# Cross attention's key products: five quarters moved from the span levels into the block attention

## The chip, the cores and the metric

One core of one Trainium2 chip runs the program. The metric is the device time of one execution in microseconds (us). Engines are named as in the profile: PE is TensorE's matmul side (PEld its weight loads), DVE is VectorE, ACT is ScalarE, POOL is GpSimd and SP is SyncE, which here issues the large weight transfers.

## What is computed

Two transformer blocks run one after the other over 256 tokens of width 1024. The first has a forgetting attention, an RWKV mixer and a mixture of 64 experts. The second has a token mixer of four groups (an mLSTM, a short convolution, a block attention called MoBA, and an HGRN2 recurrence), a cross attention over 256 memory tokens, and a gated feed-forward. The change lies in the second block. What matters of the reference:

```python
# token mixer of the second block: four independent groups of 256 columns
h_m = mlstm_chunkwise(...)                       # y_m
y_c = c_b * causal_dwconv(c_c * c_h, sconv_w)
y_a = moba_attention(a_q, a_k, a_v, rel_bias)    # 4 heads of 64, softmax over 256 keys
o_h = hgrn2_chunkwise(q_h, k_h, log_f, h_i)      # y_h
y   = concatenate([y_m, y_c, y_a, y_h]) @ w_out

# cross attention: k and v depend on the memory alone, not on x
q = xn @ wq
k = memn @ wk      # 256 x 512: the "key products"
v = memn @ wv      # 256 x 512
```

The keys `k` and values `v` of the cross attention need only the normalised memory and their weights. They can be computed at any time before the cross attention's scores, and the kernel uses them as work for PE while other groups wait for each other.

## The kernel before, in words

Every engine has one hand-written instruction stream, and semaphores order them. Nothing is reordered at run time: what stands first in an engine's stream holds up all that stands behind it. In the stretch of interest PE runs, in this order:

1. The mLSTM's heads (`weights`, `weighted`), then the transposes of the block attention's queries and keys.
2. **The block attention.** `moba_scores(h)` makes the scores of head h (two products with the head's keys, two that add the bias; 8 matmul records). `moba_attend(h)` issues five identity products (`keep_warm(5, 0)`, whose results nobody reads), waits for the exponentials of head h (`w_exp`, from ACT), transposes the three probability tiles, issues two more identity products, waits for DVE's copy of the transposes (`tp_evac`) and multiplies with the values. The scores of head h+1 are issued ahead of `moba_attend(h)`. On DVE, head h+1's scores are copied (L3254), two maxima are taken (L3256, L3257), and then the transposes of head h are copied (`moba_copy`, L3247). ACT takes the exponentials (L1178, L1180).
3. **The span levels** of HGRN2, eight of them (levels 0 to 7; `LEVELS` is 7). In each level PE issues `span_sums(level + 1)` (L2095), one quarter of the key or value products, the four transposes of the level's rows (L1361; they wait for DVE's `ft_src`), another quarter, and, once DVE has copied the transposes to `fT` (L3113), the level's products (L2120, L2122 in level 7). In each level DVE copies the transposes (L3113), makes the rows of the next level (`level_source`: L3279, L3284), does a piece of other work (`beside_level`: convolution taps, convolution sums, the mLSTM's norm and gate) and adds the masked products (L3308, L3310, twice each). ACT takes one exponential per level (`span_exp`, L1188).
4. The mixing products over `w_mix_out` (L1334), and later the cross attention.

`keys_values_part(n)` is one of sixteen quarters: n from 0 to 3 make the first half of the keys (`(J_CK, 0)`), 4 to 7 the second half, 8 to 11 and 12 to 15 the two tiles of the values (`J_CV`). A quarter is four matmuls over half of the depth, shown as 8 records of 256 columns (L1976, keys) or 4 of 512 (L1334, values). The first quarter of an output waits for its bank to be copied out (`lin_evac`) and, for keys and values each once, for their weights (`w_full`). ACT copies the finished outputs out of PSUM with `lin_copy_heads` (keys) and `lin_copy` (values). The ring of weights has two slots: SP loads `w_mix_out`'s first half into the slot of `w_ck` once the keys are done, and its second half into the slot of `w_cv` once the values are.

A score bank (`score_bank`, banks 6 and 7), a transpose bank (4 and 5) and the output banks 2 and 3 aren't touched by the quarters, which go to banks 0 and 1. The identity products go to bank 0.

Of the kernel before, what the change touches and what calls it, by code (L numbers as in the profile page):

```python
# [141 lines left out]
def build(nc, A, consts, out):  # L142
# [22 lines left out]
    with ctx:  # L165
# [222 lines left out]
        ckT = silu_c[:, :, :].rearrange("p (h b) c -> p h (b c)", h=CH)  # L388
# [221 lines left out]
        outputs = {}  # L610
# [20 lines left out]
        J_CK, J_CV, J_MIX = (J_OUT + 2 + i for i in range(3))  # L631
# [33 lines left out]
        def lin_bank(o):  # L665


            first = outputs[(J_OUT, 0)]
            if first <= o < first + 2 * T:
                return o - first  # L670
            return o % 2 + 6 * (o in [outputs[(("row", i), 0)] for i in range(N_ROWS)])

        def after(j, t=0):

            return outputs[(j, t)] + 1
# [155 lines left out]
        def _(act):  # L831
# [21 lines left out]
            def rstd(dst, src):  # L853

                rstd_n[0] += 1
                act.wait_ge(inv_var, rstd_n[0])
                act.activation(dst, src, ACT.Sqrt).then_inc(rstd_done, 1)

            def lin_copy(j, t, dst):
                act.wait_ge(lin_mm, after(j, t))  # L860
                act.activation(dst, bank[lin_bank(outputs[(j, t)])][:, 0:jobs[j][2]], ACT.Copy).then_inc(lin_evac, 1)

            def lin_copy_heads(j, i, dst):

                act.wait_ge(lin_mm, after(j, i))
                act.activation(dst[:, 2 * i:2 * i + 2, :],
                               bank[outputs[(j, i)] % 2][:, :].rearrange("p (h c) -> p h c", h=2), ACT.Copy)\
                    .then_inc(lin_evac, 1)
# [41 lines left out]
            for t in range(T):  # L910
                act.wait_ge(lin_mm, after(J_LORA, t))
                b = bank[lin_bank(outputs[(J_LORA, t)])]
                lo, n = IN_JOBS[J_LORA]
# [216 lines left out]
            for i in range(N_IN2):  # L1130
# [3 lines left out]
                for t in range(T):  # L1134
                    act.wait_ge(lin_mm, after(("in2", i), t))
                    n = in2_width(i)
# [46 lines left out]
            def span_exp(level):  # L1183

                act.wait_ge(decay_mm, GH + level + 1)
                if level >= 2:
                    act.wait_ge(ft_src, level - 1)
                act.activation(ex2[:, level % 2, :], bank[2 + level % 2][:, :], ACT.Exp).then_inc(hg_exp, 1)  # L1188

            span_exp(0)  # L1190
            for level in range(LEVELS + 1):
                if level < LEVELS:
                    span_exp(level + 1)
                if level in (1, 3):
                    lin_copy_heads(J_CK, level // 2, ckT)
                if level == 5:
                    rstd(ms[:, 12, :], ms[:, 11, :])
                if level in (5, 7):
                    lin_copy(J_CV, level // 2 - 2, cv[:, level // 2 - 2, :])
# [111 lines left out]
        def _(pe):  # L1311
# [5 lines left out]
            def keep_warm(n, b, lo=0, width=P):  # L1317

                for _ in range(n):
                    pe.matmul(bank[b][:, lo:lo + width], cst["ident"][:, :], cst["ident"][:, 0:width],  # L1320
                              start=True, stop=True, skip_group_check=True)

            def dense_tile(j, t, lhs, tiles=T, bias=False, part=(0, 1), bank_free=False):


                kind, lo, n, kt, parts, _ = jobs[j]
                if t == 0 and part[0] == 0:
                    full[j % RING] += 16 * len(parts)
                    pe.wait_ge(w_full[j % RING], full[j % RING])
                o = outputs[(j, t)]  # L1330
                if o >= 2 and part[0] == 0 and not bank_free:
                    pe.wait_ge(lin_evac, o - 1)
                for k in range(kt * part[0] // part[1], kt * (part[0] + 1) // part[1]):
                    mm = pe.matmul(bank[lin_bank(o)][:, 0:n], lhs(k, t), ring[:, j % RING, k * n:(k + 1) * n],  # L1334
                                   start=(k == 0), stop=(k == kt - 1 and not bias))
                if part[0] < part[1] - 1:
                    return
                if bias:
                    mm = pe.matmul(bank[lin_bank(o)][:, 0:n], ones[0:1, :],
                                   ring[0:1, j % RING, KT * BANK:KT * BANK + n], start=False, stop=True)  # L1340
                mm.then_inc(lin_mm, 1)
# [600 lines left out]
            for u in range(2, 2 * N_IN2):  # L1942
# [19 lines left out]
                if u % 2 == 0:  # L1962
                    mm.then_inc(in_done, 1)

            def dense_T_quarter(j, i, quarter):

                h, first = quarter // 2, quarter % 2 * KT // 2
                o = outputs[(j, i)]
                if quarter == 0:
                    if i == 0:  # L1970
                        full[j % RING] += 16 * len(jobs[j][4])
                        pe.wait_ge(w_full[j % RING], full[j % RING])
                    pe.wait_ge(lin_evac, o - 1)
                for k in range(first, first + KT // 2):
                    lo = k * CW + (2 * i + h) * CHD
                    mm = pe.matmul(bank[o % 2][:, h * 2 * P:(h + 1) * 2 * P], ring[:, j % RING, lo:lo + CHD],  # L1976
                                   xT[:, k, :], start=(k == 0), stop=(k == KT - 1))
                if quarter == 3:
                    mm.then_inc(lin_mm, 1)

            def keys_values_part(n):

                i, quarter = n // 4, n % 4
                if i < 2:
                    dense_T_quarter(J_CK, i, quarter)
                else:
                    dense_tile(J_CV, i - 2, xTk, part=(quarter, 4))
# [24 lines left out]
            n = tp_n[0]  # L2012
# [45 lines left out]
            def moba_scores(h):  # L2058
                b = score_bank()
                pe.matmul(b[:, 0:P], head_of(qT2, h, 0, P), head_of(kT2, h, 0, P), start=True, stop=False)  # L2060
                pe.matmul(b[:, 0:P], cst["anti"][:, :], hankel[:, h, P:2 * P], start=False, stop=True)
                pe.matmul(b[:, P:3 * P], head_of(qT2, h, P, 2 * P), head_of(kT2, h), start=True, stop=False)
                pe.matmul(b[:, P:3 * P], cst["anti"][:, :], hankel[:, h, :], start=False, stop=True).then_inc(sc_mm, 1)

            def moba_attend(h):
                keep_warm(5, 0)
                pe.wait_ge(w_exp, GH + h + 1)
                transposes([(i * P, (i + 1) * P, P, pr2[:, h % 2, i * P:(i + 1) * P]) for i in range(3)])
                keep_warm(2, 0)
                pe.wait_ge(tp_evac, TP_P2 + h + 1)  # L2070
                c = slice(h * HD, (h + 1) * HD)
                v = lambda t: z2[:, t, A_V + h * HD:A_V + (h + 1) * HD]
                w = lambda i: wT2[:, h % 2, i * P:(i + 1) * P]
                pe.matmul(bank[2][:, c], w(0), v(0), start=True, stop=True)
                pe.matmul(bank[3][:, c], w(1), v(0), start=True, stop=False)
                pe.matmul(bank[3][:, c], w(2), v(1), start=False, stop=True).then_inc(o_mm, 1)

            moba_scores(0)
            pe.wait_ge(o_used, 1)
            for h in range(GH):  # L2080
                if h + 1 < GH:
# [20 lines left out]
            for level in range(LEVELS + 1):  # L2102
                if level < LEVELS:
                    span_sums(level + 1)
                keys_values_part(2 * level)
                pe.wait_ge(ft_src, level + 1)
                transposes([((2 * pair + t) * P, (2 * pair + t + 1) * P, P,
                             level_rows[level % 2][:, t, pair * P:(pair + 1) * P])
                            for pair in range(2) for t in range(T)])
                keys_values_part(2 * level + 1)  # L2110
                pe.wait_ge(tp_evac, TP_HG + level + 1)
                for parity in range(2):
                    b = score_bank()
                    r = slice(HD * parity, HD * parity + HD)
                    for pair in range(2):
                        if level < LEVELS:
                            for t in range(T):
                                i = 2 * pair + t
                                f = fT[r, pair, t * P:(t + 1) * P]
                                mm = pe.matmul(b[:, i * P:(i + 1) * P], f, f, start=True, stop=True)  # L2120
                        else:
                            mm = pe.matmul(b[:, pair * P:(pair + 1) * P], fT[r, pair, 0:P], fT[r, pair, P:2 * P],  # L2122
                                           start=True, stop=True)
                    mm.then_inc(sc_mm, 1)
# [1372 lines left out]
```

## Time and profile before

| | us |
|---|---|
| Median of 3 runs | 1439.46 (1436.92 to 1439.6) |
| Profiled execution, its own time | 1441.09 |
| Its span in the trace | 1438.5 |
| PE busy in the span | 1352.1 (94%) |
| DVE busy | 640.7 (45%) |
| ACT busy | 364.2 (25%) |
| Chain that ended last, shares of the span | PE 82%, DVE 11%, DMA 3%, issue 2%, ACT 2% |

The span is what the trace covers; the profiled execution took 2.6 us more than its span. All start times below count from the span's start. The block attention lies at 1063 to 1084 us and the span levels at 1085 to 1137 us. "PE busy" counts everything that PE runs, the identity products too, so it doesn't tell what PE's work is worth. The chain that ended last is followed back from the last instruction, at each step to what released it; only what lies on it sets the time. PEclk is the granted clock of TensorE as a share of full speed: 1.00 is 2.4 GHz and 0.50 is 1.2 GHz.

### The profile page before, as it was taken

How to read it: one execution, taken by the hardware profiler on the slowest of the kernel's cores; microseconds unless marked ns; L12 is line 12 of the kernel's file. 1: busy time of each engine (PE TensorE's matmuls, PEld its weight loads, DVE VectorE, ACT ScalarE, POOL GpSimd, SP SyncE). 2: the span in 40 equal slices, each digit the busy share in tenths (PEclk: the TensorE clock that was granted, in tenths of full speed). 3: DMA queues.
4: the chain of work that ended last, by engine and by line, in shares of the span. 5: the costliest groups of instructions: out<-in, count | busy, mean ns of one | idle time of the engine just before them, and what ended most of it. 6: DMA issues, size and time to landing. Idle time of an engine off the chain costs nothing.

```text
span 1438.5 us, 20229 instructions
## 1 busy us (share of the span) xinstructions
PE 1352.1 (94%) x8028; PEld 860.9 (60%) x8028; DVE 640.7 (45%) x1201; ACT 364.2 (25%) x624; POOL 43.9 (3%) x50
## 2 busy tenths in 40 slices
PE   5998988999889999999999999899999998999997
PEld 2535446875544444444444444568778566899985
DVE  2136357627632222222222222465347843777763
ACT  0202240020111222212212222245321112345542
POOL 0014200000000000000000000300000000000000
PEclk9999999969899999999999999999979999999999
DMA  9774275006529999999999997935530231355552
GB/s 340 238 231 144 73 300 228 3 1 242 236 97 400 419 420 415 416 420 406 415 418 421 414 416 290 312 132 160 163 27 21 97 118 59 117 177 191 190 178 85
DMA packets 94536, 339.10 MB, mean 236 GB/s; under 512 B 8736, under 2 KB 42168, under 8 KB 65677
## 3 DMA queue, kind: packets, MB, share of 16 engines
q1 hardware_dynamic: 84192, 319.06, 57.8%
q10 hardware_dynamic: 8109, 12.33, 3.5%
q0 software_dynamic: 2176, 6.86, 1.4%
q8 instruction: 45, 0.74, 0.2%
q14 instruction: 14, 0.11, 0.0%
HBM read 333.22 MB, written 1.05 MB: 232 GB/s over the span
## 4 chain that ended last, share of the span: by engine, by line
PE 82%; DVE 11%; DMA 3%; issue 2%; ACT 2%; ACTq 0%; DVEq 0%
PE bank L1847 16%; PE bank L1334 10%; PE bank L1863 8%; PE bank L1349 6%; PE bank L1350 6%; PE bank L1351 6%; PE bank L1810 3%; PE bank L1811 2%; PE bank L1828 2%; PE bank L1830 2%; DMA small<-in_norm_g 2%; PE bank L1320 2%; PE bank L1361 2%; DMA ring<-in_w_in 1%; PE bank L1747 1%
## 5 line engine op out<-in xcount | busy, mean ns | idle before, releaser
L1334 PE MATMUL bank<-ring,xT 128*128 128x512 f32 (+1 forms) x416 | 183.4, 598 | 7.1 <-DMA ring<-in_w_in 3.0
L1334 PEld LDWEIGHTS bank<-ring,xT 128*128 128x128 f32 x416 | 80.6, 196 | 97.8 <-issue 86.2
L1863 PE MATMUL bank<-dn,tmp 128*64 128x512 f32 x528 | 120.6, 598 | 0.0
L2924 DVE TENSOR_TENSOR xT<-bank,mod 128x512 fp32r<-128x512 f32 x66 | 45.7, 692 | 157.9 <-ACT mod L1084 150.7
L2917 DVE SCALAR_TENSOR_TENSOR tmp<-silu_c,rc,bank 128x256 f32<-128x256 f32 x33 | 22.6, 684 | 196.7 <-ACT silu_c L1071 191.4
L1349 PE MATMUL bank<-mod,w_high 128*128 128x256 f32 x352 | 98.6, 280 | 1.7 <-DVE xT L3424 1.7
L1350 PE MATMUL bank<-xT,w_high 128*128 128x256 f32 x352 | 98.6, 280 | 0.0
L1351 PE MATMUL bank<-mod,ring 128*128 128x256 f32 x352 | 98.2, 279 | 0.0
L3411 DVE TENSOR_TENSOR ring<-ring,w_high 128x1024 fp32r<-128x1024 f32 x66 | 77.8, 1221 | 22.0 <-ACT w_high L1269 20.3
L1320 PE MATMUL bank<-c_ident 128*128 128x128 f32 (+1 forms) x568 | 76.0, 285 | 0.0
L1863 PEld LDWEIGHTS bank<-dn,tmp 128*64 128x64 f32 x528 | 35.0, 136 | 68.3 <-issue 68.3
L1320 PEld LDWEIGHTS bank<-c_ident 128*128 128x128 f32 x568 | 71.6, 200 | 6.0 <-issue 5.3
L1084 ACT ACTIVATE mod<-bank 128x512 fp32r<-128x512 f32 x64 | 38.2, 597 | 133.8 <-PE bank L1863 133.8
L1269 ACT ACTIVATE w_high<-ring 128x1024 fp32r<-128x1024 f32 x66 | 65.8, 1049 | 22.8 <-DMA ring<-in_w_ffn_out 22.8
L1810 PE MATMUL bank<-mod,gains 128*128 128x256 f32 x272 | 70.1, 296 | 0.5 <-ACT gains L1052 0.5
L1349 PEld LDWEIGHTS bank<-mod,w_high 128*128 128x128 f32 x352 | 66.6, 189 | 2.1 <-issue 1.9
L1810 PEld LDWEIGHTS bank<-mod,gains 128*128 128x128 f32 x272 | 51.5, 189 | 26.9 <-issue 26.2
L1071 ACT ACTIVATE silu_c<-bank 128x256 f32<-128x256 f32 x32 | 12.3, 384 | 217.8 <-PE bank L1847 217.8
L1811 PE MATMUL bank<-mod,xn 128*128 128x256 f32 x272 | 66.3, 282 | 0.0
L1351 PEld LDWEIGHTS bank<-mod,ring 128*128 128x128 f32 x352 | 66.0, 188 | 0.0
L1350 PEld LDWEIGHTS bank<-xT,w_high 128*128 128x128 f32 x352 | 65.9, 187 | 0.0
L1847 PE MATMUL bank<-ring,gains 128*64 128x512 f32 x272 | 62.1, 599 | 1.4 <-ACT gains L1058 1.4
(653 smaller groups left out, 2311.9 us busy)
## 6 DMA issues: line engine op xcount, KB each, us to landing
dn<-in_exp_w_down SPq DMA_DIRECT2D x66, 1024.0 KB, 10.3
ring<-in_exp_w_gate SPq DMA_DIRECT2D x34, 1024.0 KB, 9.3
ring<-in_exp_w_up SPq DMA_DIRECT2D x34, 1024.0 KB, 11.4
gu_odd<-in_exp_w_gate SPq DMA_DIRECT2D x32, 1024.0 KB, 9.7
gu_odd<-in_exp_w_up SPq DMA_DIRECT2D x32, 1024.0 KB, 11.8
ring<-in_w_ffn_in SPq DMA_DIRECT2D x22, 1024.0 KB, 5.1
ring<-in_ada_w SPq DMA_DIRECT2D x16, 1024.0 KB, 6.5
ring<-in_w_in SPq DMA_DIRECT2D x7, 2048.0 KB, 10.6
```

The costliest lines, as they stand in the source:

```text
L1269: act.activation(of_unit(w_high, u, q, PIECE), of_unit(ring, u, q, PIECE), ACT.Copy)\
L1320: pe.matmul(bank[b][:, lo:lo + width], cst["ident"][:, :], cst["ident"][:, 0:width], start=True, stop=True, skip_group_check=True)
L1334: mm = pe.matmul(bank[lin_bank(o)][:, 0:n], lhs(k, t), ring[:, j % RING, k * n:(k + 1) * n], start=(k == 0), stop=(k == kt - 1 and not bias))
L1349: pe.matmul(out, w[0], x[0], start=start, stop=False, skip_group_check=True)
L1350: pe.matmul(out, w[0], x[1], start=False, stop=False, skip_group_check=True)
L1351: return pe.matmul(out, w[1], x[0], start=False, stop=stop, skip_group_check=True)
L1810: pe.matmul(out_k, xn_high[:, t, k * P:(k + 1) * P], pick[:, t, :], start=(t == 0), stop=False)
L1811: mm = pe.matmul(out_k, xn_low[:, t, k * P:(k + 1) * P], pick[:, t, :], start=False, stop=(t == T - 1))
L1847: mm = pe.matmul(bank[4][CHUNKS[c], :], hg_k[:, CHUNKS[c]], gate_up_of(gu_w(c), k), start=(k == 0), stop=(k == KT - 1))
L1863: mm = pe.matmul(bank[6 + h][CHUNKS[c], :], act_eT[:, 0, k, CHUNKS[c]], dn[:, 2 * parity + c, lo:lo + BANK], start=(k == 0), stop=(k == D_ ...
L2924: dve.tensor_tensor(y_low[:, c], bank[6 + h][:, :], y_high[:, c].bitcast(F32), ALU.subtract)\
L3411: dve.tensor_tensor(at_piece(w_low), at_piece(ring), at_piece(w_high).bitcast(F32), ALU.subtract)\
```

## The change

In the block attention the five identity products at the head of `moba_attend(h)` are replaced by one quarter of the keys (quarters 1 to 4 for heads 0 to 3), and quarter 0 goes between the scores of head 0 and the wait for `o_used` that stands ahead of the scores of head 1. The two identity products later in `moba_attend` stay for heads 0 to 2, now in the bank of the second half of the keys, which isn't begun yet; for head 3 they are dropped. In the span levels the eleven quarters that are left stand as `PARTS_AT` says: two each in levels 0, 2 and 4, one in each of the others, always ahead of the transposes where there is only one. ACT copies out the first half of the keys right behind the first exponential (was: in level 1) and the second half in level 1 (was: in level 3). The copies of the values stay where they were.

```diff
--- before.py
+++ after.py
@@ -1188,11 +1188,12 @@
                 act.activation(ex2[:, level % 2, :], bank[2 + level % 2][:, :], ACT.Exp).then_inc(hg_exp, 1)
 
             span_exp(0)
+            lin_copy_heads(J_CK, 0, ckT)
             for level in range(LEVELS + 1):
                 if level < LEVELS:
                     span_exp(level + 1)
-                if level in (1, 3):
-                    lin_copy_heads(J_CK, level // 2, ckT)
+                if level == 1:
+                    lin_copy_heads(J_CK, 1, ckT)
                 if level == 5:
                     rstd(ms[:, 12, :], ms[:, 11, :])
                 if level in (5, 7):
@@ -1962,6 +1963,8 @@
                 if u % 2 == 0:
                     mm.then_inc(in_done, 1)
 
+            PARTS_AT = ((5, 6), (7,), (8, 9), (10,), (11, 12), (13,), (14,), (15,))
+
             def dense_T_quarter(j, i, quarter):
 
                 h, first = quarter // 2, quarter % 2 * KT // 2
@@ -2063,10 +2066,11 @@
                 pe.matmul(b[:, P:3 * P], cst["anti"][:, :], hankel[:, h, :], start=False, stop=True).then_inc(sc_mm, 1)
 
             def moba_attend(h):
-                keep_warm(5, 0)
+                keys_values_part(h + 1)
                 pe.wait_ge(w_exp, GH + h + 1)
                 transposes([(i * P, (i + 1) * P, P, pr2[:, h % 2, i * P:(i + 1) * P]) for i in range(3)])
-                keep_warm(2, 0)
+                if h + 1 < 4:
+                    keep_warm(2, lin_bank(outputs[(J_CK, 1)]))
                 pe.wait_ge(tp_evac, TP_P2 + h + 1)
                 c = slice(h * HD, (h + 1) * HD)
                 v = lambda t: z2[:, t, A_V + h * HD:A_V + (h + 1) * HD]
@@ -2076,6 +2080,7 @@
                 pe.matmul(bank[3][:, c], w(2), v(1), start=False, stop=True).then_inc(o_mm, 1)
 
             moba_scores(0)
+            keys_values_part(0)
             pe.wait_ge(o_used, 1)
             for h in range(GH):
                 if h + 1 < GH:
@@ -2102,12 +2107,14 @@
             for level in range(LEVELS + 1):
                 if level < LEVELS:
                     span_sums(level + 1)
-                keys_values_part(2 * level)
+                for n in PARTS_AT[level][0:1]:
+                    keys_values_part(n)
                 pe.wait_ge(ft_src, level + 1)
                 transposes([((2 * pair + t) * P, (2 * pair + t + 1) * P, P,
                              level_rows[level % 2][:, t, pair * P:(pair + 1) * P])
                             for pair in range(2) for t in range(T)])
-                keys_values_part(2 * level + 1)
+                for n in PARTS_AT[level][1:]:
+                    keys_values_part(n)
                 pe.wait_ge(tp_evac, TP_HG + level + 1)
                 for parity in range(2):
                     b = score_bank()
```

## Rows read from the trace of the kernel before

**Rows 1.** The chain that ended last, in both stages: start, us, engine, tile, line.
```profile
1073.18 1.11 PE bank L1320 x10
...
1104.47 0.70 DVE z L3284
```

**Rows 2.** Timeline of PE, block attention: start, us, engine, line, operation, count [idle before].
```profile
1065.96 0.49 PE L2060 MATMUL bank<-kT,qT 64*128 64x128 f32 x2
...
1069.07 0.49 PE L1361 MATMUL bank<-c_ident,pr 128*128 128x128 f32 x3
...
1073.02 1.28 PE L1320 MATMUL bank<-c_ident 128*128 128x128 f32 x10
1074.13 0.49 PE L1361 MATMUL bank<-c_ident,pr 128*128 128x128 f32 x3
1074.46 0.61 PE L1320 MATMUL bank<-c_ident 128*128 128x128 f32 x4
```

**Rows 3.** Timeline of ACT, ends of the exponentials of heads 0 and 1.
```profile
1068.22 0.19 ACT L1180 ACTIVATION_READ_ACCUMULATOR pr<-sc,ms 128x1 f32 x1
...
1070.31 0.18 ACT L1180 ACTIVATION_READ_ACCUMULATOR pr<-sc,ms 128x1 f32 x1
```

**Rows 4.** Timeline of DVE, block attention.
```profile
1064.15 0.88 DVE L3202 TENSOR_TENSOR xn<-bank,ms 128x256 f32<-128x256 f32 x2
...
1074.13 0.41 DVE L3257 TENSOR_REDUCE ms<-sc 128x1 f32<-128x256 f32 x1
1074.66 0.56 DVE L3247 COPY wT<-bank 128x384 f32<-128x384 f32 x1
```

**Rows 5.** Timeline of PE, span levels 0 and 1.
```profile
1087.25 1.89 PE L1976 MATMUL bank<-xT,ring 128*128 128x256 f32 x8
1088.97 0.60 PE L1361 MATMUL bank<-c_ident,hg 128*128 128x128 f32 x4
1089.41 1.89 PE L1976 MATMUL bank<-xT,ring 128*128 128x256 f32 x8
1091.23 1.71 PE L2120 MATMUL bank<-fT 64*128 64x128 f32 x16
...
1093.84 1.89 PE L1976 MATMUL bank<-xT,ring 128*128 128x256 f32 x8
...
1097.83 1.71 PE L2120 MATMUL bank<-fT 64*128 64x128 f32 x16
```

**Rows 6.** Timeline of DVE, span levels: the copies of levels 0, 1, 2 and 7.
```profile
1089.61 0.69 DVE L3113 COPY fT<-bank 128x512 f32<-128x512 f32 x1 [1.64 <-PE bank L1361]
...
1096.28 0.69 DVE L3113 COPY fT<-bank 128x512 f32<-128x512 f32 x1 [1.53 <-PE bank L1361]
...
1099.88 0.69 DVE L3308 TENSOR_TENSOR tmp<-bank,c_level_t 128x512 f32<-128x512 f32 x1
...
1103.08 0.69 DVE L3113 COPY fT<-bank 128x512 f32<-128x512 f32 x1 [0.22 <-DVE mod L3310]
...
1136.02 0.69 DVE L3113 COPY fT<-bank 128x512 f32<-128x512 f32 x1 [0.22 <-DVE mod L3310]
```

**Rows 7.** Timeline of SP's queue, and transfers with sizes and us to landing.
```profile
1022.68 0.37 SPq L740 DMA_DIRECT2D ring<-in_w_ck  x1
...
ring<-in_w_ck SPq DMA_DIRECT2D x1, 2048.0 KB, 8.4
```

**Rows 8.** Busy us and instructions of each engine in four stretches, then PEclk, DMA.
```profile
1096.30:1136.00 39.70, 39.57 (x211) 27.98 (x210) 35.13 (x59) 7.44 (x11) 0.00 (x0) 1.00 0.16 54
...
1190.00:1206.00 16.00, 12.81 (x91) 11.63 (x92) 7.98 (x15) 5.57 (x17) 0.00 (x0) 1.00 0.42 133
...
1044.00:1060.00 16.00, 14.97 (x53) 12.05 (x52) 7.77 (x18) 5.09 (x10) 1.16 (x3) 0.51 0.70 56
1036.00:1044.00 8.00, 6.40 (x40) 4.44 (x39) 6.82 (x15) 6.36 (x8) 1.52 (x3) 1.00 0.99 219
```

**Rows 9.** Timeline of PE, identity products in the mLSTM's stage.
```profile
1051.65 1.65 PE L1320 MATMUL bank<-c_ident 128*128 128x128 f32 x6
```

## The prediction

> **What bounds the kernel now.** The page gives PE 94% busy, which alone would say that any work taken from PE is won. I read the chain that ended last first, over the two stages that the change touches, and it tells two different things. In the block attention it lies on PE and passes through the five identity products of each head [rows 1]. In the span levels it lies on DVE from level 1 to level 7: L3279, L3284, L3308, L3310, level after level [rows 1]. Then I read the timelines of PE, ACT and DVE against each other to see who has slack in each stage.
>
> Block attention. PE never stops for long: the scores of head 1 begin at 1065.96 and the transposes of head 0 at 1069.07 [rows 2]. For head 1 the five identity products begin at 1073.02 and the transposes at 1074.13, with no idle time noted before them, although ACT had finished that head's exponentials at 1070.31 + 0.18 = 1070.5 [rows 2, 3]. So the wait at which the identity products stand isn't one for ACT. What they do cover is DVE: it still has to reduce the scores of the next head, until 1074.13 + 0.41 = 1074.54, before it can copy the transposes at 1074.66 [rows 4]. The transposes take 0.33 (1074.13 to 1074.46 [rows 2]), plus the drain of the last one. Both sides of that copy, PE's transposes and DVE's reduction, come in within about a tenth of a us. The 1.11 us of identity products (1073.02 to 1074.13) fill this cover exactly, and there is nothing left of it for anything longer.
>
> Span levels. PE shows as busy for 39.57 of 39.70 us, DVE for 35.13 [rows 8], so the busy shares point at PE again. But DVE's idle time says otherwise. It waits for PE's transposes twice, 1.64 us in level 0 and 1.53 us in level 1; from level 2 to level 7 the copy of the transposes is preceded by 0.22 us that its own last addition ends (two of the six stand in [rows 6]). The levels' products end before DVE wants them as well: those of level 1 begin at 1097.83 [rows 5] and last 1.71 (as in level 0), to 1099.54, and DVE takes them at 1099.88, straight behind its own convolution sums [rows 6]. From 1096.28 to 1136.02 DVE needs 39.74 us for six levels, 6.62 each, and this is its own work. PE's full timeline there is coincidence: its two quarters happen to fill DVE's period.
>
> **The change part by part.**
>
> *Quarters taken out of the levels.* The price of a quarter is 1.72 us, from its start to that of the transposes behind it (1087.25 to 1088.97), or 1.82 where the level's products follow (1089.41 to 1091.23) [rows 5]. Five of them are 8.6 us of PE. In levels 0 and 1 DVE does wait for PE, but there the quarter that stands ahead of the transposes stays (quarters 5 and 7 in place of 0 and 2), and the transposes come no earlier; the second quarter of level 1, which goes, stands behind them. In levels 2 to 7 DVE is the one that is late. So none of the 8.6 us is on the path: they become idle time of PE ahead of each level's products. Gain: 0. Bounds: below nothing isn't possible by work taken away (the clock aside, below); a gain could at most reach the idle time that DVE shows for other causes, six times 0.22 = 1.3 us [rows 6], and I take 0 because the level's transposes ended well before DVE asked in the later levels.
>
> *Quarter 0 between the scores of heads 0 and 1.* Behind it PE waits for `o_used`, which DVE gives after L3202, at 1064.15 + 0.88 = 1065.03 [rows 4], ahead of the 1065.96 at which PE goes on now [rows 2]. No wait there hides it. Queued behind it are the scores of head 1, on which DVE's next copy and both exponentials of head 1 hang, and the transposes of head 0, for which ACT was ready at 1068.22 + 0.19 = 1068.4 [rows 3] against 1069.07. At most 0.66 us of slack that belongs to this head is lost in front; none can be won. Cost: +1.72 (bound 1.82).
>
> *Quarters 1 to 4 in place of the five identity products.* Each costs 1.72 - 1.11 = 0.61 us [rows 2, 5]. The cover is used up, as said, so all of it falls on the path: 4 x 0.61 = +2.44. The busy times of the rows, 1.89 and 1.28, give the same 0.61. Bounds: 0.51 each, if the tenth of a us between the two sides of DVE's copy can be won, and 0.71 with the 1.82; 2.0 to 2.8.
>
> *The last two identity products of head 3 dropped.* After the transposes PE waits for DVE's copy anyway: in head 1 they begin at 1074.46 and last 0.61, to 1075.07, and DVE copies from 1074.66 to 1075.22 [rows 2, 4]. They lie under the copy. Gain: 0.
>
> *The weights.* Quarter 0 now wants `w_ck` some 21 us sooner. It was issued at 1022.68 and took 8.4 [rows 7]: there at 1031.1, 34 us ahead. Nothing. The slot of the keys is free sooner, so the first half of `w_mix_out` starts sooner; the mixing products come after the levels, and the data was there already.
>
> *ACT.* The copy of the first half of the keys goes ahead of the second exponential. It is one 128x512 instruction, which I price by DVE's 0.69 for the same shape [rows 6], and DVE wants the second exponential only after its copy at 1089.61 and the next rows, over 1.4 us after that. Nothing. The copy of the second half waits for quarter 7 in level 1, and the next exponential behind it isn't wanted before level 2. Nothing. No DMA is moved past another on SP's queue.
>
> **The sum.** +1.72 + 2.44 - 0 = +4.16 us. The profiled execution was 1441.09 with a span of 1438.5; changed, its span would be 1442.7 and its time 1445.2. On the median of the three runs, 1439.46, this makes 1443.6. By the bounds (1.72 + 2.0 - 1.3 and 1.82 + 2.8) the forecast's own range is +2.4 to +4.6, 1441.9 to 1444.1, with about 1 us for the scatter between runs (they span 2.7 us).
>
> **The rivals.**
>
> *PE is the bound of the levels after all.* Its place is the level's products and the transposes in front of DVE's copy; its price is the whole 8.6 us off, so 4.16 - 8.6 = -4.4: 1435.0, faster. It decides from the point at which DVE waits for a record of PE in levels 2 to 7. For it: 39.57 of 39.70 us busy [rows 8], and PE's levels repeat every 6.60 us (1091.23 to 1097.83 [rows 5]), close to DVE's 6.62. Against it: not one of six copies waits for PE [rows 6], and the chain stays on DVE. The Trainium skill (Perfetto Trace Analysis, Optimization Strategies) says to keep the matmul engine as highly utilized as possible, by which real products in place of identity products should win; the same passage says to optimize the engines that block the path while PE waits, and by that half nothing is won in the levels. The trace bears out the second half. Chance 8%.
>
> *PE's clock falls in the levels.* With 8.6 us less, PE is busy for about 31 of 39.7 us, 78%. Against it: at 1190 to 1206 us PE was busy for 12.81 of 16 us and its granted clock stayed at 1.00 (2.4 GHz). For it: the stretch from 1036 to 1044, busy for 6.40 of 8 at 1.00, was followed by 16 us at 0.51, which is 1.2 GHz [rows 8], and six records of identity products took 1.65 us there [rows 9] where ten took 1.28 at full clock [rows 2]. A level with one quarter holds 6.60 - 1.82 = 4.8 us of PE, 9.6 at half clock, against DVE's 6.62: 3.0 lost per level. For 16 us, as in that stretch, that is 16 / 9.6 = 1.7 levels and +5: 1448.6. The Trainium skill (TensorE: Matmul & The Clock Gate, What's actually happening) says that the array's default is the throttled state and that activity releases it, which speaks against trading PE's density for idle time; the idle time here is in pieces of under 2 us. Chance 11%.
>
> *The change does what its name says and fits into waits.* If the quarters hid in the block attention, its cost would be near 0 and so would be the gain in the levels: 1439.5, no change. It decides where T of a head waits for ACT; ACT is 3.6 us early for head 1 (1070.5 against 1074.13), so only a cover that I overlooked would do it. Chance 6%.
>
> **How the numbers follow.** Forecast 75%, faster 8%, clock 11%, hidden 6%. The time is the forecast's, 1443.6. The range takes in the hidden case and leaves out the faster case and most of the clock case: 1439.0 to 1446.5. About 0.2%, 2.9 us, is what a measurement of this kernel can tell from no change. The forecast's +4.16 lies 1.3 us beyond that, so of its 75% I give 11 to a reading of no change and 64 to slower. With the rivals: faster 8%, same 17%, slower 75%.
>
> **What the changed profile would show.** In the block attention, 8 records of L1976 between the scores and the transposes, 1.72 long, and the transposes of successive heads 5.06 + 0.61 = 5.67 apart (now 1069.07 to 1074.13 [rows 2]). DVE's level copy of level 7 comes 4.2 us later, and the distance from level 1's copy to level 7's stays 39.7 us. PE shows some 8.6 us of new idle time in the levels, ended by DVE's L3113, with PEclk at 1.00. The prediction is wrong if the distance between those copies shrinks by more than 1 us (PE was the bound), if PEclk falls below 1.00 there, or if the transposes of successive heads stay 5.1 us apart.

## The result, and the profile after

| | before | changed |
|---|---|---|
| Median, 20 runs each | 1437.41 us | 1451.03 us |
| Lowest and highest | 1434.44 to 1446.55 | 1442.07 to 1455.68 |
| Ratio, 95% interval | 1 | 1.0077 (1.0059 to 1.0095) |
| Span of the profiled execution | 1438.5 us | 1450.7 us |
| Its own time | 1441.09 us | 1453.37 us |

The change makes the kernel 0.77% slower, about 11 us. The means of the 20 runs are 11.1 us apart, which is the ratio; the medians are 13.6 us apart, because the changed kernel's times fall into two groups (see the second and third trace below). The prediction was +4.16 us and 1443.6; the measured median lies above its range of 1439.0 to 1446.5. The direction was right and the size was not.

First the timeline of PE in the changed kernel, block attention, which answers to [rows 2] (the line numbers have moved by a few; the quarters are now L1979):

```profile
1070.97 1.89 PE L1979 MATMUL bank<-xT,ring 128*128 128x256 f32 x8
1072.70 0.49 PE L1362 MATMUL bank<-c_ident,pr 128*128 128x128 f32 x3
...
1076.64 1.89 PE L1979 MATMUL bank<-xT,ring 128*128 128x256 f32 x8
1078.37 0.49 PE L1362 MATMUL bank<-c_ident,pr 128*128 128x128 f32 x3
```

The quarters stand where the identity products stood, each 1.73 us from its start to the transposes, and the transposes of successive heads are 5.67 us apart (1072.70 to 1078.37), as predicted. Below is the same engine in the levels, products of levels 1, 3, 6 and 7 and the transposes behind level 7, which answer to [rows 5]:

```profile
1104.18 1.71 PE L2127 MATMUL bank<-fT 64*128 64x128 f32 x16 [0.86 <-DVE fT L3120]
...
1117.78 2.28 PE L2127 MATMUL bank<-fT 64*128 64x128 f32 x16 [1.88 <-DVE fT L3120]
...
1138.18 1.71 PE L2127 MATMUL bank<-fT 64*128 64x128 f32 x16 [1.50 <-DVE fT L3120]
...
1144.39 0.72 PE L2129 MATMUL bank<-fT 64*128 64x128 f32 x8 [2.15 <-DVE fT L3120]
1145.70 1.68 PE L1362 MATMUL bank<-c_ident,xn 128*128 128x128 f32 x8 [0.58 <-DVEq L3307]
```

The work taken out of PE has become idle time (the number in brackets), which DVE's copies (L3120) end. That was predicted too. But what stands behind the idle times of 1.88 and 2.15 us runs longer: level 3's 16 records take 2.28 us in place of 1.71, and the 8 records of transposes behind level 7 take 1.68 where the kernel before needs 1.09. The table of 4-us stretches says why; its columns are the stretch, its length, the busy us (and instructions) of PE, PEld, DVE, ACT and POOL, then PEclk, the DMA share and GB/s:

```profile
1092.00:1096.00 4.00, 4.00 (x14) 3.21 (x13) 0.69 (x1) 1.68 (x3) 0.00 (x0) 0.64 0.00 0
...
1120.00:1124.00 4.00, 4.00 (x12) 2.63 (x12) 3.65 (x7) 0.60 (x1) 0.00 (x0) 0.73 0.00 2
...
1148.00:1152.00 4.00, 4.00 (x21) 4.00 (x21) 1.57 (x3) 0.00 (x0) 0.00 (x0) 0.50 0.25 88
```

Three times the granted clock of PE falls to its lower level, 1.2 GHz (PEclk 0.50; a stretch that holds both levels shows a value between): at the first span sums ahead of level 0, in levels 3 and 4, and behind level 7, where it lasts into the mixing products. In the trace of the kernel before it is 1.00 from A to G, the marks given below. DVE's copies of the transposes in levels 0, 1 and 7, to be read against [rows 6]:

```profile
1096.76 0.69 DVE L3120 COPY fT<-bank 128x512 f32<-128x512 f32 x1 [2.89 <-PE bank L1362]
...
1103.43 0.69 DVE L3120 COPY fT<-bank 128x512 f32<-128x512 f32 x1 [1.54 <-PE bank L1362]
...
1143.65 0.69 DVE L3120 COPY fT<-bank 128x512 f32<-128x512 f32 x1 [0.22 <-DVE mod L3317]
```

To add up where the time went I take seven marks from the timelines, each the start of an instruction: the first scores of the block attention (A), the last value product of head 3 (B), the first span sums (C), DVE's copy in level 1 (D) and in level 7 (E), the first mixing product (F), and PE's transposes (8 records) behind the mixing products (G). From G on to the end the two kernels agree within 0.1 us.

| stretch | before | changed | difference |
|---|---|---|---|
| start to A | 1063.90 | 1065.19 | +1.29 |
| A to B, block attention | 19.96 | 24.14 | +4.18 |
| B to C | 1.59 | 1.58 | 0 |
| C to D, levels 0 and 1 | 10.83 | 12.52 | +1.69 |
| D to E, levels 1 to 7 | 39.74 | 40.22 | +0.48 |
| E to F, level 7 to mixing | 6.36 | 9.39 | +3.03 |
| F to G, mixing products | 24.47 | 26.09 | +1.62 |
| A to G | 102.95 | 113.94 | +10.99 |

The +1.29 ahead of A lies in instructions that the change doesn't touch, and such stretches differ between any two executions; 1.05 of it comes from the mLSTM's stage, where the clock is low in both traces and was low for longer in this one. A to G is +10.99. That this is so near to the ratio (0.0077 of 1437 is 11.1) is partly luck: two more traces of the same kernel, below, have +9.30 and +5.01. Of the 10.99, 4.18 is the price of the quarters in the block attention and 6.8 stands in stretches in which PE's clock fell.

### The profile page after: what moved, and what is told of

Same layout as the page of the kernel before. It is cut to its first block, busy times and chain, and to the rows that moved or that the text cites. A ratio compares the mean times of both kernels' runs of the same rounds, so it can differ in the third digit from the quotient of the medians.

```text
span 1450.7 us, 20141 instructions
## 1 busy us (share of the span) xinstructions
PE 1361.0 (94%) x7984; PEld 868.5 (60%) x7984; DVE 639.7 (44%) x1201; ACT 364.1 (25%) x624; POOL 44.8 (3%) x50
## 3 DMA queue, kind: packets, MB, share of 16 engines
HBM read 333.22 MB, written 1.05 MB: 230 GB/s over the span
## 4 chain that ended last, share of the span: by engine, by line
PE 82%; DVE 11%; DMA 3%; issue 2%; ACT 1%; ACTq 0%; DVEq 0%
PE bank L1848 16%; PE bank L1335 10%; PE bank L1864 8%; PE bank L1350 6%; PE bank L1351 6%; PE bank L1352 6%; PE bank L1811 3%; PE bank L1812 2%; PE bank L1829 2%; PE bank L1831 2%; DMA small<-in_norm_g 2%; PE bank L1321 2%; PE bank L1362 2%; DMA ring<-in_w_in 1%; PE bank L1936 1%
```

## The experiments

The theory, once the result and its trace were known: (1) the change costs 4.2 us in the block attention, on PE's path; (2) it wins nothing in the levels, since DVE bounds them; (3) the idle time that it leaves on PE lets the granted clock fall, and the work behind runs at half speed. The rivals: the falls have nothing to do with the idle time; the quarters cost something of their own beyond their length; PE bounds the levels. Each kernel was timed beside the kernel before on the same chip, and each ratio is to that kernel; the changed kernel was not timed again beside them. The stages come from each kernel's trace by the marks above. An identity product is a matmul that only keeps PE busy; its result isn't read.

### The idle time filled in the levels (e1_fill_levels)

Eight identity products go into each level that lost a quarter (against the changed kernel):

```diff
+                b = score_bank()
+                if len(PARTS_AT[level]) == 1:
+                    keep_warm(8, 6 + (sc_n[0] - 1) % 2)
                 pe.wait_ge(tp_evac, TP_HG + level + 1)
                 for parity in range(2):
-                    b = score_bank()
+                    b = score_bank() if parity else b
```

> The changed kernel with eight identity products put into each of the five levels that lost their second quarter (levels 1, 3, 5, 6, 7), ahead of the level's own products. PE's idle time there is filled, nothing else changes. Theory (the idle time lets the clock fall): PEclk is 1.00 from the first level's transposes on to the mixing products; the fall that the changed kernel shows ahead of the first level stays, since nothing is filled there. About 5 us less than the changed kernel, 6 more than the kernel before (1.004). Rival (the falls have nothing to do with the idle time): falls at about 1117 and 1145 us stay, and the time is that of the changed kernel (1.008). Rival (PE bounds the levels): the filling costs what the quarters did, and the time is above the changed kernel's.

Measured: ratio 1.0026 (1.0008 to 1.0045), 5 points of a thousand below the changed kernel's 1.0077. Busy time of the engines from A to G, with PEclk, of this kernel:

```profile
1058.41:1165.51 107.10, 104.04 (x537) 73.24 (x537) 68.69 (x127) 18.34 (x41) 0.00 (x0) 1.00 0.13 45
```

and of the changed kernel:

```profile
1065.19:1179.13 113.94, 103.49 (x456) 70.39 (x457) 68.71 (x127) 18.39 (x40) 0.00 (x0) 0.93 0.12 42
```

PEclk is 1.00 all through. D to E is 39.72, E to F 6.36, F to G 24.48, as in the kernel before; A to B stays at 24.13. The added products cost nothing, so they lie under DVE's work: PE doesn't bound levels 2 to 7. The copying of the keys and the start of the weights' transfer stand where the changed kernel has them (36.03 us behind A, against 37.72 with the fall ahead of level 0), so they aren't what lets the clock fall. One part was expected otherwise: the fall ahead of level 0 should have stayed, as nothing was filled there, and C to D is 10.83 without it. That fall comes and goes (see the second and third trace below), so its 1.69 us, which are part of the 6.84 between the two traces, aren't what the filling gave back; 5.1 are.

### The last head's two identity products put back (e2_head3), and both (e3_both)

e2 is the changed kernel with this edit; e3 has it together with e1's.

```diff
-                if h + 1 < 4:
-                    keep_warm(2, lin_bank(outputs[(J_CK, 1)]))
+                keep_warm(2, lin_bank(outputs[(J_CK, 1)]) if h + 1 < 4 else 6)
```

> The changed kernel with the two identity products of the last head in the block attention put back (into a free bank). Theory (their loss, with the wait for DVE ahead of the first level, let the clock fall at about 1091 us): PEclk stays at 1.00 through the first level, the stretch from the last head's products to the copy of level 1 is 1.7 us shorter, and the falls later in the levels stay: about 1.5 us less than the changed kernel. Rival (off the path, no effect): the fall at about 1091 stays and the times are equal.

> Both fillings together: the changed kernel's order of work without its new idle time. Theory (the change costs 4.2 us in the block attention, and the rest is clock): PEclk 1.00 from 1065 us to the mixing products, block attention 23.6 us long, level 1's copy to level 7's 39.7 us; 4.2 us over the kernel before, ratio 1.003. Rival (something else in the moved quarters costs time): the ratio stays near 1.008.

Measured: e2 1.0051 (1.0030 to 1.0073), e3 1.0032 (1.0013 to 1.0051). In e2 C to D is 10.83, but D to E is 40.21, E to F 9.31 and F to G 26.18: the later falls are all there. In e3 A to G is

```profile
1062.94:1170.05 107.11, 104.49 (x540) 73.73 (x541) 68.70 (x127) 18.34 (x41) 0.00 (x0) 1.00 0.13 45
```

4.16 us over the 102.95 of the kernel before, all of it in A to B (24.14, where 23.6 was expected). With the clock held, the change costs what the sum of the prediction said. e2's trace agrees with the story of the last head, but the traces that follow take it away again. e2's ratio lies 2.6 points of a thousand below the changed kernel's, and their intervals overlap; whether the two products make falls rarer stays open.

### Two more traces of the changed kernel (after_again, after_third)

> The changed kernel as it is, a second look at its trace. Theory (the loss is PEclk's falls, set by PE's idle time): block attention 24.1 us, one or more falls between 1088 and 1150 us, copy of level 1 to copy of level 7 at or a little above 39.7. If the missing identity products of the last head cause the fall ahead of the first level, it is there again; if that one was chance, first span sums to level 1's copy is 10.8 us now.

> The changed kernel as it is, a third look at its trace. Theory (idle time in the levels): the falls in levels 3 and 4 and behind level 7 are there for the third time, and the mixing products lose about 4.6 us; the fall ahead of the first level, seen in one of two looks, may be there or not.

The two executions took 1452.95 and 1445.57 us. C to D was 10.83 in both: the fall ahead of level 0 was seen in one trace of three, with the same instructions each time, so the missing identity products of head 3 are neither needed for it nor enough (a run below, e6, has them and has the fall). The record shows one thing that goes with it. The stretch from the product with `c_bucket` ahead of the mLSTM to A takes 32.19 us in the first trace of the changed kernel and 32.17 in e6, the two with this fall, and 30.8 to 31.2 in the nine other traces in which the mLSTM's stage is as before. The mLSTM's own low clock lasted longer in those two. Whether that brings on the later fall wasn't tried. The fall in the middle levels was there each time. The one behind level 7 was there in the second trace (E to F 9.36, F to G 26.13) and, against the expectation, not in the third (6.37 and 24.47). In the third the clock had fallen earlier, in level 6, and for a short time:

```profile
1134.69 2.10 PE L2127 MATMUL bank<-fT 64*128 64x128 f32 x16 [1.50 <-DVE fT L3120]
...
1141.25 0.72 PE L2129 MATMUL bank<-fT 64*128 64x128 f32 x8 [0.86 <-DVE fT L3120]
```

Level 6's products took 2.10 us, level 7's quarter behind them ended later, and only 0.86 us of idle time was left ahead of level 7's products, where the first trace had 2.15. The clock was back before the mixing products, and PE's idle time in the levels took most of the slow stretch: A to G is 107.96, +5.0 in place of +11.0. e4 below shows the same, a fall right behind level 6's products, 0.86 us ahead of level 7's and none behind level 7; the three traces without a fall in level 6 and with both last levels emptied (the first two here and e2) have 2.15 and the fall behind level 7. So three traces of the same program have 5, 9 and 11 us more than before between A and G, by where the falls land. The 20 timed runs have such a spread: six lie between 1442.1 and 1445.9, twelve between 1450.4 and 1455.7, two between. That the falls make these two groups fits the three traces, whose executions took 1453.37, 1452.95 and 1445.57 us; the other timed runs have no trace.

### Five quarters left out, block attention as before (e4_eleven)

This kernel is the kernel before without the five quarters that the change takes out of levels 1, 3, 5, 6 and 7; it leaves part of the keys and values uncomputed. (One flag that closes an accumulation is set earlier, where its last part is missing; not shown.)

```diff
+            PARTS_AT = ((0, 2), (3,), (4, 6), (7,), (8, 11), (12,), (14,), (15,))
...
-                keys_values_part(2 * level)
+                for n in PARTS_AT[level][0:1]:
+                    keys_values_part(n)
...
-                keys_values_part(2 * level + 1)
+                for n in PARTS_AT[level][1:]:
+                    keys_values_part(n)
```

> The kernel before with five of its sixteen quarters left out of the computation (the same five places in levels 1, 3, 5, 6, 7 that the change empties), and the block attention as it was. Part of the keys and values isn't computed. Theory (DVE bounds levels 2 to 7, and idle time lets the clock fall): no gain from 8.6 us less of PE work; level 1's copy to level 7's stays at 39.7 us or above, falls of PEclk in the later levels or the mixing products, 0 to 5 us more than the kernel before (1.000 to 1.0035). Rival (PE bounds the levels): 8.6 us less, 0.994.

Measured: 1.0000 (0.9980 to 1.0021). PE's busy time from A to G is down by 5 us (100.12 in the kernel before; 8.6 us of products are gone, and what runs at the lower clock takes longer), and nothing is won:

```profile
1067.29:1171.18 103.89, 95.17 (x472) 65.33 (x473) 68.67 (x127) 18.56 (x41) 0.00 (x0) 0.97 0.13 46
```

Against the 102.95 of before, A to G is 0.94 longer. D to E grew to 40.67 from 39.74, with idle times of 1.86 and 1.50 us ahead of the products of levels 3 and 6 and PEclk below 1.00 behind each. This parts the change: its second half alone, the emptier levels, is worth nothing at best. It also shows that the falls in the levels don't need the quarters in the block attention.

### More identity products in the block attention (e5_ident)

```diff
-                keep_warm(5, 0)
+                keep_warm(8, 0)
                 pe.wait_ge(w_exp, GH + h + 1)
...
             moba_scores(0)
+            keep_warm(8, 0)
```

> The kernel before with more identity products in the block attention and nothing else: eight in place of five in each head, and eight between the scores of heads 0 and 1. Theory (PE's order there is the path, whatever the products are): the stage grows by 8 x 0.22 = 1.8 plus 4 x 3 x 0.22 = 2.7, 4.4 us in all, the levels stay full and their length at 39.7 us, PEclk stays at 1.00 from the block attention to the mixing products; ratio 1.003. Rival (the quarters cost something that identity products don't, the bank or the weights): under 3 us.

Measured: 1.0017 (0.9997 to 1.0036). A to B is 24.43, 4.47 more than before; the other stretches are those of before within 0.01 and PEclk is 1.00. The first half of the change is priced by its length, whatever runs there. The timed ratio reaches from none to 5 us and can't decide alone; the trace does.

### The last two levels filled (e8_fill_last_two)

The edit is shown against e1:

```diff
-                if len(PARTS_AT[level]) == 1:
+                if level in (6, 7):
                     keep_warm(8, 6 + (sc_n[0] - 1) % 2)
```

> The changed kernel with eight identity products in levels 6 and 7 alone, ahead of the level's products. Theory (the fall behind level 7, which slows the mixing products, comes from PE's idle time in the last two levels): level 7's copy to the first mixing product is 6.4 us in place of 9.4 and the mixing products up to the next transposes 24.5 in place of 26.1; the fall in levels 3 and 4 stays and costs its 0.5 us, so 4.6 us less than the changed kernel. Rival (the idle time of all levels adds up): the fall is put off or stays, and less than 2 us come back.

Measured: 1.0026 (1.0007 to 1.0046). E to F is 6.37 and F to G 24.47, D to E 40.27: the fall in levels 3 and 4 is there, its products again behind 1.91 us of idle time,

```profile
1113.10 2.29 PE L2130 MATMUL bank<-fT 64*128 64x128 f32 x16 [1.91 <-DVE fT L3123]
```

and the one behind level 7 isn't. As the third trace of the changed kernel shows, one trace without it would prove little; the timed ratio, 5 points below the changed kernel's, and its ten times, none above 1447.9 us, suggest that it is gone from most runs. Sixteen identity products in levels 6 and 7 do the work of the forty in e1, as far as the time can tell: they don't keep the clock up everywhere, but where products come next that PE bounds.

### Two quarters moved, and no more (e6_two_moved)

Against the kernel before, only heads 2 and 3 get a quarter, and levels 0 and 1 keep one quarter each, behind the transposes. (The two later identity products of every head stay, in another bank; not shown.)

```diff
             def moba_attend(h):
-                keep_warm(5, 0)
+                if h < 2:
+                    keep_warm(5, 0)
+                else:
+                    keys_values_part(h - 2)
...
-                keys_values_part(2 * level)
+                if level >= 2:
+                    keys_values_part(2 * level)
+                elif level == 0:
+                    keep_warm(3, 6)
                 pe.wait_ge(ft_src, level + 1)
...
-                keys_values_part(2 * level + 1)
+                keys_values_part(2 * level + 1 if level >= 2 else 2 + level)
```

> The kernel before with only two quarters moved into the block attention, in place of the five identity products of heads 2 and 3, and levels 0 and 1 holding one quarter each, behind the transposes (before: two each, one ahead of them); levels 2 to 7 as before, three identity products ahead of level 0's transposes. Theory (DVE waits for PE only in levels 0 and 1, and only for the quarter ahead of the transposes): block attention +1.2 us, first span sums to level 1's copy 2.3 us shorter, level 1's copy to level 7's 39.7, no fall of PEclk: 1 us less than the kernel before, which the stage lengths show and the time (0.999) can't. Rival (the levels are PE's after all): 39.7 shrinks. Rival (no gain in levels 0 and 1): 1.2 us more.

Measured: 0.9988 (0.9970 to 1.0005). A to B is 21.18 (+1.22), D to E 39.74, as expected. C to D is 10.15 in place of the 8.5 expected: the clock fell ahead of level 0, with head 3's identity products in their place. The span sums, 8 records, took 3.65 us, where the kernel before needs 1.97. The time alone can't tell this kernel from the one before; the stages give -0.7 from C to D and +1.2 from A to B:

```profile
1080.10 0.61 PE L1320 MATMUL bank<-c_ident 128*128 128x128 f32 x4
...
1082.99 3.65 PE L2098 MATMUL bank<-hg,c_span 128*128 128x256 f32 x8 [1.20 <-DVEq L3275]
```

### The mLSTM's waits filled (e7_warm_mlstm)

The kernel before has a fall of its own [rows 8], ahead of the stretch of the change. Does idle time matter there too?

```diff
-            transpose_all(mem, layer=4)
+            transpose_all(mem, layer=4, tiles=(0,))
+            keep_warm(3, 0)
+            transpose_all(mem, layer=4, tiles=(1,))
+            keep_warm(3, 0)
...
             pair_transposes(M_K)
-            keep_warm(3, 0)
+            keep_warm(5, 0)
...
+            keep_warm(3, 0)
             pe.wait_ge(tp_evac, TP_ML + 3)
...
-                keep_warm(3, 2, 3 * P)
+                keep_warm(3 if h else 8, 2, 3 * P)
```

> The kernel before with identity products in the waits ahead of and in the mLSTM's first head (three behind each tile's transposes of the memory, two more ahead of the wait for the row maxima, three ahead of the last wait, five more in head 0), where PEclk falls to 0.50 for some 16 us in every look so far. Theory (idle time and small matmuls let the clock fall there, as idle time does in the changed kernel): PEclk stays at 1.00 through the stage and the whole is 3 to 6 us shorter, 0.997. Rival (idle time isn't what matters there): PEclk falls all the same and the added products cost up to 2 us.

Measured: 0.9982 (0.9961 to 1.0004). The fall came later and was shorter. From the bias product (the `c_bucket` product) ahead of the mLSTM to A, before and in this kernel:

```profile
1032.76:1063.90 31.14, 28.13 (x139) 22.44 (x139) 17.86 (x41) 13.37 (x21) 2.68 (x5) 0.73 0.68 102
```

```profile
1032.37:1062.58 30.21, 28.97 (x172) 24.05 (x171) 17.89 (x41) 13.39 (x21) 2.69 (x5) 0.83 0.70 105
```

The 16 added products show as 33 more records, and the stretch is 0.9 us shorter at a mean clock of 0.83 in place of 0.73. That is less than the 3 to 6 us expected, the timed ratio can't tell it from no change, and it is no proof yet.

### Both, with all waits filled (e9_filled, e9_again)

e6 and e7 together (against the kernel before; only what neither has is shown), with nine and six identity products in the mLSTM's heads 0 and 1, and five ahead of the first span sums:

```diff
-                keep_warm(3, 2, 3 * P)
+                keep_warm((9, 6, 3, 3)[h], 2, 3 * P)
...
+            keep_warm(5, 6)
             pe.wait_ge(hg_act, 3)
             pe.wait_ge(o_used, 2)
             span_sums(0)
```

> The kernel with two quarters moved, with its waits filled: five identity products ahead of the first span sums, and in the mLSTM's stage those of the run on that stage, with nine in head 0 and six in head 1 (before: three each). Theory: no fall at the first level, first span sums to level 1's copy 8.5 us (10.8 in the kernel before), block attention 21.2, copy of level 1 to copy of level 7 39.7; the mLSTM's fall put off further or gone. 2 to 5 us less than the kernel before, 0.998. Rival (the fall at the first level comes from the small products ahead of it, not from the idle time): it is there in spite of the filling and the stretch is over 10 us.

> The kernel with two quarters moved and its waits filled, a second look at its trace. Theory: PEclk stays at 1.00 through the mLSTM's stage again (27.2 us from the bias product to the block attention's first scores, 31.1 in the kernel before) or falls late in it, at the shorter identity runs of heads 2 and 3; span sums to level 1's copy 8.7 us. Rival (the first look was chance): a fall for 10 to 16 us and 29 us or more.

Measured: 1433.25 against 1439.34 us on the same chip, ratio 0.9965 (0.9944 to 0.9986). The second traced execution took 1427.93 us, 7.9 less than the first, all of it ahead of the bias product. From there to G both traces agree within 0.01 us in every stretch and show no fall, where each of the twelve traces of the other kernels has one in the mLSTM's stage. The bias product to A, and A to G, in the first:

```profile
1032.41:1059.56 27.15, 25.85 (x179) 21.34 (x179) 17.89 (x41) 13.37 (x21) 2.68 (x5) 1.00 0.76 117
```

```profile
1059.56:1161.58 102.02, 99.97 (x496) 68.21 (x497) 68.70 (x127) 18.58 (x41) 0.00 (x0) 1.00 0.14 47
```

4.0 us come from the mLSTM's clock (31.14 to 27.15). Of the moved quarters, +1.23 in A to B against -2.14 in C to D (8.69) leaves -0.9. Together 4.9, and the ratio says 5.0. By its ratio this version is faster than the kernel before, and so than the changed one. It doesn't tell the fillings apart.

## Why the prediction was wrong, point by point

**Block attention, +1.72 + 4 x 0.61 = +4.16: right.** Measured +4.18 in the first trace of the changed kernel and +4.18 in e3. The reading that the identity products filled their cover exactly held: in the changed kernel DVE waits 0.74 us for PE's transposes in each of heads 0 to 2, where both came in within a tenth of a us before. The head 3 products were rightly priced at nothing in their own place.

**Levels, gain 0 from the work taken out: right.** D to E is 39.72 to 39.74 wherever the clock held, with full levels (before, e5) or with levels filled by identity products (e1, e3), and e4 wins nothing by leaving the work out. The rival that PE is the bound, given 8%, is refuted: 39.57 of 39.70 us busy was no sign of it.

**The clock: the step that failed.** The sum put the clock at nothing: the levels' "Gain: 0" set it aside, and it stood only as a rival with 11% and 1448.6. It is what happened. In the first trace the falls cost 6.8 us beside the 4.18: 1.69 ahead of level 0, 0.48 in levels 3 and 4, and 4.65 (3.03 + 1.62) behind level 7. Both the chance and the price were wrong.

The chance was kept low by one row, the stretch at 1190 to 1206 us that was busy for 12.81 of 16 us at PEclk 1.00, and on the remark that the idle time would be in pieces of under 2 us. The idle time came as single waits of 0.86 us (level 1), 0.16 (level 2), 1.88 (level 3), and 0.86, 1.50 and 2.15 in levels 5 to 7, one quarter each, where it grows; in level 7, which has no span sums for a next level, it went above 2 us. In every trace with emptied levels that weren't all filled, at least one fall followed (the changed kernel three times, e2, e4, e8); with the levels filled there was none (e1, e3). How long the single waits are doesn't settle it either, as two lines of the kernel before show, the longest wait of PE at 1036 to 1044 and the longest at 1190 to 1206:

```profile
1036.93 1.16 PE L1361 MATMUL bank<-c_ident,mod 128*128 128x128 f32 x8 [0.51 <-DVE xT L2342]
...
1194.03 0.66 PE L1361 MATMUL bank<-c_ident,prx 128*128 128x128 f32 x4 [1.20 <-ACT prx L1230]
```

Both stretches are busy for 80%. The first, with waits of 0.25 to 0.51 us, was followed by a fall; the second, with waits of 0.34 to 1.20 us, had none. So the second stretch couldn't keep the chance low: the first has the same busy share and the opposite outcome.

The price was 3.0 us per level, +5 in all, for a fall of 16 us in the levels. In fact the fall in levels 3 and 4 lasted under 4 us and cost 0.5, since the idle time of PE on both sides of it took the rest. The one ahead of level 0 lasted under 4 us too and cost 1.69, since there DVE waits for PE. The one that cost 4.65 began in level 7 and ran on for some 10 us, into the small products and the mixing products, where PE is the bound; that stage wasn't in the sum.

**The range.** It left out most of the clock case. The three runs that it started from were also a little high: their median is 1439.46, that of 20 runs 1437.41. With the falls as the first trace has them, the same sum gives 1439.46 + 10.99 = 1450.4, which the range had to reach.

**What stays open.** What decides whether a given stretch of idle time is followed by a fall. The same program had the fall ahead of level 0 in one trace of three and the one behind level 7 in two of three. e9 shows no fall in two traces, with three fillings made at once; which of them is needed wasn't tried.

## What to carry to other kernels

Work moved off an engine that isn't the bound wins nothing, and on PE it can lose: the idle time it leaves can be followed by a lower clock for the PE-bound work that comes after, in another stage than the one changed. Before taking products out of a stage, write down the single waits that will be left in it and what follows them, and fill them with identity products where they cost nothing (e1 gave back 7 of the 11 us by the timed ratios without any other change). Identity products that just fill a cover aren't free room: what replaces them must be no longer than they are.

## What the runs showed of the hardware that I had not expected

The granted clock depends on details that a mean busy share hides. PE was busy for 80% of 1036 to 1044 us in the kernel before, and the clock fell; it was busy for 80% of 1190 to 1206 us, and the clock stayed. Filling the waits of the first stretch and of the mLSTM's heads behind it kept it at 2.4 GHz through the whole stage of 27 us in two traces (e9), with all the stage's own matmuls as they were. A fall may also keep the next one away: in the third trace of the changed kernel and in e4 a short fall behind level 6's wait made PE slower, and so less idle ahead of level 7 (0.86 us in place of 2.15), and the expensive fall behind it didn't come. That is two traces against three, and it wasn't tested by an edit of its own. And a program with the same instructions can have two typical times, here about 8 us apart, 1442 to 1446 and 1450 to 1456; the three traces fit the falls as their cause.
